# A two-model decoder on one core: order of the weight rounding at its nine boundaries, norm offset, first tile, end and a memory bank

## The reference

```
for l in range(2):
    x = x + 0.5 * rms_norm(swiglu(rms_norm(x)), w)           # ffn1, width 2816
    x = x + rms_norm(parallel_head_groups(rms_norm(x)), w)   # retention + gated DeltaNet ("mix")
    x = x + rms_norm(cross_attention(rms_norm(x), rms_norm(mem)), w)
    x = x + 0.5 * rms_norm(swiglu(rms_norm(x)), w)           # ffn2
h = rmsnorm(x) @ w_in        # second model: Mamba2 branch and dilated attention branch
x = x + (gates0 * y_ssm + gates1 * y_att) @ w_mix_out
x = x + swiglu(rmsnorm(x))
return rmsnorm(x)            # final norm, scaled by norm_final
```

## Time and profile before

| | |
|---|---|
| median of three runs | 1930.05 us |
| the profiled execution's own time | 1928.99 us |
| its span, first to last instruction | 1927.2 us |
| granted TensorE clock, mean | 0.997 of full speed |
| PEld / DVE / ACT / POOL busy | 87% / 37% / 56% / 80% |
| POOL, line 390 (`wlo`) | 1184 instructions, mean 1310 ns, 1501.8 us |
| ACT, line 417, `whi` | 299 instructions, mean 1902 ns |
| the chain that ended last | PE 94%, ACT 3%, DVE 2% of the span |

### The profile page before, as it was taken

One profiled execution on the slowest core, in us unless ns is written; L12 is line 12 of the kernel. 1 busy time (PEld: TensorE's weight loads), 2 busy tenths in 40 slices (PEclk: granted clock), 3 DMA queues, 4 the chain that ended last, 5 costly groups with the idle time before them and its releaser, 6 DMA issues.

```text
span 1927.2 us, 28342 instructions
## 1 busy us (share of the span) xinstructions
PE 1910.8 (99%) x11287; PEld 1683.6 (87%) x11287; DVE 708.3 (37%) x1406; ACT 1087.2 (56%) x1458; POOL 1544.8 (80%) x1227
## 2 busy tenths in 40 slices
PE   9999999999999999999999999999999999999998
PEld 7888899988888888889999888888999998888887
DVE  2221767521211222138574231113676632122112
ACT  6645674456644575456734665446666667545443
POOL 6998786666899799979776759997767787888995
PEclk9999999999999999999999999999999999999999
DMA  8554543143655565555323536555443444545552
GB/s 320 191 193 173 203 148 132 49 179 124 221 195 192 183 228 198 189 183 195 134 88 110 193 113 217 182 192 212 152 158 136 153 154 153 178 177 202 197 187 98
DMA packets 48661, 331.50 MB, mean 172 GB/s; under 512 B 5393, under 2 KB 6289, under 8 KB 10514
## 3 DMA queue, kind: packets, MB, share of 16 engines
q1 hardware_dynamic: 44208, 314.61, 45.1%
q10 hardware_dynamic: 4322, 15.09, 2.2%
HBM read 328.63 MB, written 1.05 MB: 171 GB/s over the span
## 4 chain that ended last, share of the span: by engine, by line
PE 94%; ACT 3%; DVE 2%; ACTq 1%; issue 0%; DVEq 0%; DMA 0%
PE bank L1942 20%; PE bank L1911 16%; PE bank L1912 16%; PE bank L1913 16%; PE bank L1946 10%; ACT arena L417 1%; PE bank L2050 1%; PE bank L2074 1%; PE bank L2386 1%; PE bank L2402 1%; PE bank L2016 1%; PE bank L2052 1%; PE bank L2508 1%; PE bank L2647 1%; PE bank L2487 1%
## 5 line engine op out<-in xcount | busy, mean ns | idle before, releaser
L390 POOL TENSOR_TENSOR wlo<-raw,whi 128x512 fp32r<-128x512 f32 x1184 | 1501.8, 1310 | 332.6 <-ACT whi L417 332.0
L417 ACT ACTIVATE whi<-raw 128x2048 fp32r<-128x2048 f32 (+1 forms) x299 | 568.1, 1902 | 192.0 <-PE bank L1913 156.6
L417 ACT ACTIVATE arena<-bank 128x512 f32<-128x512 f32 (+4 forms) x389 | 210.8, 552 | 439.8 <-PE bank L1946 266.4
L1942 PE MATMUL bank<-uT,whi 128*128 128x512 f32 x1632 | 408.2, 392 | 0.0
L1942 PEld LDWEIGHTS bank<-uT,whi 128*128 128x128 f32 x1632 | 296.3, 189 | 55.0
L1946 PEld LDWEIGHTS bank<-uT,wlo 128*128 128x128 f32 x1632 | 222.6, 190 | 15.9
L1946 PE MATMUL bank<-uT,wlo 128*128 128x256 f32 x1632 | 227.5, 282 | 0.0
L1911 PE MATMUL bank<-uT,whi 128*128 128x256 f32 x768 | 222.6, 290 | 0.3 <-DVE memT L1221 0.3
L1912 PE MATMUL bank<-uT,whi 128*128 128x256 f32 x768 | 217.1, 283 | 0.0
L1913 PE MATMUL bank<-uT,wlo 128*128 128x256 f32 x768 | 217.1, 283 | 0.0
L1911 PE MATMUL bank<-whi,uT 128*128 128x512 f32 (+1 forms) x416 | 160.8, 387 | 0.0
(11 more groups left out here) (315 smaller groups left out, 2698.6 us busy)
## 6 DMA issues: line engine op xcount, KB each, us to landing
raw<-in_w SPq DMA_DIRECT2D x295, 1024.0 KB, 4.8
rows<-in_rows ACTq DMA_DIRECT2D x22, 512.0 KB, 4.9
raw<-in_w SPq DMA_DIRECT2D x4, 512.0 KB, 7.2
arena<-in_mem ACTq DMA_DIRECT2D x2, 1024.0 KB, 9.5
x<-in_x SPq DMA_DIRECT2D x2, 512.0 KB, 5.4
out<-x SPq DMA_DIRECT2D x2, 512.0 KB, 2.7
arena<-in_amask ACTq DMA_DIRECT2D x1, 576.0 KB, 6.1
cst<-in_cst SPq DMA_DIRECT2D x1, 468.0 KB, 10.9
```

The source lines that it names most:

```text
L390: r = pool.tensor_tensor(wlo[n % LAND][:, k], raw[n % LAND][:, k], whi[n % RING][:, k].bitcast(F32), ALU.subtract)
L417: return act.activation(o, i, f, **k)
L1942: pe.matmul(both, w[0][:, c], parts[:, :, k, :], start=start and k == 0, stop=False)
```

## The change

Edit A is in `boundary`: ACT no longer rounds a weight unit between `pre_root(1)` and the rounding of tile 1; it rounds two behind it. Edit B: in `pre_root`, DVE makes mean plus epsilon (`pre_bias`) in place of ACT, and ACT waits for it in front of the root. Edit C: PE gets four more idle products after the first two products of the first tile and two more in the middle of it. Edit D: the last piece of `y_part` goes to bank 4, with a wait for the first `m_ready`, and ACT and DVE take it right behind the other three. Edit E, the end: DVE scales tile 0 in two halves between the adds of tile 1; for tile 1 POOL multiplies one half with the norm weights and ACT scales it, and DVE does the other half, into `ub`; each store starts when both halves of its tile are ready. Edit F: three semaphores of early tables become one (`tables_in`), and `cleared` becomes `pool_side`.

```diff
@@ boundary (ACT) @@
                 pre_root(1)
-                split()
                 u_hi(1)
-                split()
+                split(2)
@@ sum_root (ACT) @@
-                    act.drain()
-                    if h == 0:
+                    d = act.drain()
+                    if h == 0 and done == "rms_pre":
+                        d.then_inc(sems["pre_sum"], 1)
+                    elif h == 0:
                         fn(st[:, c0 + 4 + t:c0 + 5 + t], st[:, c0 + t:c0 + t + 1], AF.Identity, scale=1.0 / n, bias=eps)
+                if done == "rms_pre":
+                    act.wait_ge(sems["norm_dve"], p.count("norm_dve"))
@@ pre_scale (DVE) @@
+            def pre_bias(t):
+                dve.wait_ge(sems["pre_sum"], p.count("pre_sum"))
+                ts(st[:, 52 + t:53 + t], st[:, 48 + t:49 + t], 1.0 / D, EPS, ALU.mult, ALU.add)\
+                    .then_inc(sems["norm_dve"], 1)
             def pre_scale(t, w):
+                pre_bias(t)
@@ first_pair (PE) @@
                     part_phase(wa, 0, a, 0, 0, (0, 1))
+                    idle_products(4)
                     pe.wait_ge(sems["w_hi"], 1)
...
                     lo_phase(wa, a, 0, 0, True)
+                    idle_products(2)
                     pe.wait_ge(sems["u_hi"], p.count("u_hi"))
@@ Mamba part: ACT, DVE, PE @@
-                        hi_parts(mT, (6, 1, 7))
+                        hi_parts(mT, (6, 1, 7, 4))
...
-                    if hp == 2 and g == 2:
-                        hi_parts(mT, (6,), 3)
...
-                        lo_parts(mT, (6, 1, 7))
-                        lo_parts(mT, (6,), 3)
+                        lo_parts(mT, (6, 1, 7, 4))
...
-                    y_part((6,), 3)
+                    pe.wait_ge(sems["m_ready"], p.n["m_ready"] + 1)
+                    y_part((4,), 3)
@@ end: POOL, ACT, DVE @@
+            pool.tensor_tensor(ub[:, 1, 0:512], x[:, 1, 0:512], rows[:, r % 3, 0:512], ALU.mult).then_inc(sems["pool_side"], 1)
...
+            act.wait_ge(sems["pool_side"], DEPTH + 1)
+            act.wait_ge(sems["norm_dve"], p.count("norm_dve"))
+            fn(ub[:, 1, 0:512], ub[:, 1, 0:512], AF.Copy, scale=st[:, 55:56]).then_inc(sems["out_ready"], 1)
...
+            stt(x[:, 0, 0:512], x[:, 0, 0:512], st[:, 54:55], w[:, 0:512], ALU.mult, ALU.mult).then_inc(sems["out_ready"], 1)
+            row_add(1, 0, N_UNITS - 1)
+            stt(x[:, 0, 512:], x[:, 0, 512:], st[:, 54:55], w[:, 512:], ALU.mult, ALU.mult).then_inc(sems["out_ready"], 1)
+            row_add(1, 1, N_UNITS - 1)
+            pre_bias(1)
+            dve.drain()
+            tt(ub[:, 1, 512:], x[:, 1, 512:], w[:, 512:], ALU.mult)
+            dve.wait_ge(sems["rms_pre"], p.count("rms_pre"))
+            dve.reciprocal(st[:, 55:56], st[:, 55:56]).then_inc(sems["norm_dve"], 1)
+            dve.drain()
+            ts(ub[:, 1, 512:], ub[:, 1, 512:], st[:, 55:56], None, ALU.mult).then_inc(sems["out_ready"], 1)
```

More of the change, by code:

```diff
@@ L347, in _ @@
             sp.dma_start(raw[2][:], a["w"][2]).then_inc(sems["raw_landed2"], 16)
-            sp.dma_start(cst[:, P:], a["cst"][:, P:]).then_inc(sems["cst_in"], 16)
-            sp.dma_start(posi, a["pos"].to_broadcast((P, SEQ))).then_inc(sems["pos_in"], 16)
-            sp.dma_start(lvl_f32, a["lvl"]).then_inc(sems["lvl_in"], 16)
+            sp.dma_start(cst[:, P:], a["cst"][:, P:]).then_inc(sems["tables_in"], 16)
+            sp.dma_start(posi, a["pos"].to_broadcast((P, SEQ))).then_inc(sems["tables_in"], 16)
+            sp.dma_start(lvl_f32, a["lvl"]).then_inc(sems["tables_in"], 16)
             for n in range(3, N_UNITS):
@@ L355, in _ @@
                 sp.dma_start(raw[n % LAND][:], a["w"][n]).then_inc(sems[f"raw_landed{n % LAND}"], 16)
-            for t in range(NT):
-                sp.wait_ge(sems["out_ready"], t + 1)
-                sp.dma_start(out[0, t * P:(t + 1) * P, :], x[:, t, :]).then_inc(sems["stored"], 16)
+            sp.wait_ge(sems["out_ready"], 2)
+            sp.dma_start(out[0, 0:P, :], x[:, 0, :]).then_inc(sems["stored"], 16)
+            sp.wait_ge(sems["out_ready"], 4)
+            sp.dma_start(out[0, P:SEQ, :], ub[:, 1, :]).then_inc(sems["stored"], 16)
             sp.wait_ge(sems["stored"], 16 * NT)
@@ L393, in _ @@
                 if n == 8:
-                    pool.wait_ge(sems["cst_in"], 16)
+                    pool.wait_ge(sems["tables_in"], 48)
                     for i, m in enumerate((UI, UI, LI, LI)):
                         pool.tensor_copy(msk4[:, i, :], m)
-                    pool.wait_ge(sems["lvl_in"], 16)
+                    pool.wait_ge(sems["tables_in"], 48)
                     pool.tensor_copy(lvl[:, :], lvl_f32)
@@ L408, in _ @@
                     score_masks()
+            r = N_ROWS - 1
+            pool.wait_ge(sems[f"row_landed{r % 3}"], 16 * (r // 3 + 1))
+            pool.wait_ge(sems["x_part2"], 4 * DEPTH + 2)
+            pool.tensor_tensor(ub[:, 1, 0:512], x[:, 1, 0:512], rows[:, r % 3, 0:512], ALU.mult).then_inc(sems["pool_side"], 1)
         @block.scalar
@@ L1270, in rotary_angles @@
             def rotary_angles():
-                dve.wait_ge(sems["cst_in"], p.count("cst_in", 16))
-                dve.wait_ge(sems["pos_in"], p.count("pos_in", 16))
+                dve.wait_ge(sems["tables_in"], 48)
+                dve.wait_ge(sems["tables_in"], 48)
                 dve.drain()
@@ L1883, in _ @@
             w = use_row()
[L1884 to L1892, removed]
+            row_add(0, 0, N_UNITS - 1)
+            row_add(0, 1, N_UNITS - 1)
+            pre_bias(0)
+            dve.wait_ge(sems["rms_pre"], p.count("rms_pre"))
+            dve.reciprocal(st[:, 54:55], st[:, 54:55])
+            dve.drain()
[6 more added lines that the diff above has]
+            tt(ub[:, 1, 512:], x[:, 1, 512:], w[:, 512:], ALU.mult)
+            dve.wait_ge(sems["rms_pre"], p.count("rms_pre"))
+            dve.reciprocal(st[:, 55:56], st[:, 55:56]).then_inc(sems["norm_dve"], 1)
+            dve.drain()
+            ts(ub[:, 1, 512:], ub[:, 1, 512:], st[:, 55:56], None, ALU.mult).then_inc(sems["out_ready"], 1)
         @block.tensor
@@ L2232, in _ @@
                 if L == 0:
-                    pe.wait_ge(sems["cst_in"], 16)
+                    pe.wait_ge(sems["tables_in"], 48)
                 first_pair((0, 1), ("tok_out", "tok_out"))
```

6 lines of the change are left out of this document (3 added, 3 removed).

## The result

The changed kernel takes 1944.47 us (median; single runs 1940.29 to 1948.15), the kernel before in the same comparison 1929.99. The ratio is 1.0074, 95% interval 1.0062 to 1.0086: slower by 14.5 us where 5.8 were predicted, and outside the range. The four runs were 1940.29, 1941.80, 1947.13 and 1948.15, so the median lies in a gap between two pairs, and no run was near it. The profiled execution took 1941.8, its span is 1940.0.

The account below looks back on a forecast made before the run. PE, 99% busy, was taken as the bound, with POOL next at 80%. +8.1 - 0.8 - 0.8 - 0.8 = +5.7 on the profiled 1928.99 gave 1934.7, or 1935.8 us against the median; range 1931 to 1939.

Parts of the forecast that it names:

- Edit A at mix and cross-attention: Boundaries into mix: PE late on POOL by +2.1 us (first layer) and +2.4 (second); into cross-attention +1.6 each, two times.
- Edit A into feed-forward parts: Into ffn2 twice and from first layer into second: gain and stall cancel, +0.1 us each, 0.3 together.
- Edit A in front of the second model: Boundary before the second model: PE's margins are above 3 us, so the transposes' gain stays, -0.35 us.
- Sum of edit A's late starts: All nine boundaries: +8.1 us net of what PE's transposes gain, bounds 7.0 to 9.2.
- Edits B to E: Transposes' wait: 0.45 us gained once, 0.2 elsewhere, counted within edit A; program start, memory bank and end: -0.8 each.
- the wait that I had named as late next: Row sums' write to bank 4, now waiting for the fourth piece's rest; edit D as a whole put at -0.8 us.
- The third rival, the clock: Clock falls in PE's new waits of about 2 us at four places; one or two falls: 1938.5 to 1942; chance 0.12.
- The step that failed outright: POOL beside DVE's SBUF work at ffn1 to mix: slowed, not fully blocked; a unit takes 6.05 us instead of 5.11.
- Edit F: 0: Early tables' semaphores: the tables land many us before anyone asks, so 0.

Follow-up runs that it names:

- the last two experiments: Changed kernel with the small multiply's operand in PSUM, 1941.84 us; the same plus eight idle products in each of the four long waits, 1940.40 us.
- The last kernel: Changed kernel with the small multiply's operand in PSUM and eight idle PE products in each of the four long waits: 1940.40 us, ratio 1.0051.

## Why the prediction was wrong

The direction and the main place were right; the size was not. Of the 8.7 us between forecast and median, some 2.6 are DVE shut out by POOL, 2.1 late starts priced too low, 1.4 the clock, 1.4 too much gain from B to E, and 1.3 the time at which the clock first rose. By steps:

- **Edit A at mix and cross-attention: right.** Against the kernel without edit A my terms amount to 2.1 + 0.45 and 2.4 + 0.2 for mix (with the gain of edit B, which they had netted) and 1.6 + 0.2 for cross-attention. Measured 2.60, 2.62 and 2.01. POOL started 3.84 behind the transposes, not 3.61, but its first unit at mix was shorter than I took.
- **Edit A into feed-forward parts: mis-sized.** "+0.1 each" plus the lost 0.2 gives 0.3, measured 0.6 to 0.66 each. The 0.23 of POOL's later start is a part of it. The other is a wait that I had passed over: the second unit there (`rows_unit`) also comes late, by 0.28. I had called the third unit the tightest and priced it alone; two margins drawn on by the same delay both have to be worked out.
- **Edit A in front of the second model: the sign was wrong.** "PE's margins are above 3 us there, the gain stays" looked at PE's margins on POOL. PE waited for DVE instead: a small `SCALAR_TENSOR_TENSOR` on SBUF operands took 0.80 to 0.84 us in every profile with edit A at this place and 0.26 to 0.28 without it; POOL now ran beside it, and it ended 0.09 behind POOL's current instruction. +0.56, where my terms come to -0.15.
- **Sum of edit A's late starts**: 10.1 by my terms, 12.2 measured.
- **Edits B to E: too much gain.** I had 2.05 for B, 0.8 each for C, D and E: 4.45. The medians say 3.0. By the starts of the kernel without A and C, the transposes gain 1.5 (0.42 once, about 0.15 at seven others) and D 0.5: the two waits go (-0.84, -0.39), and +0.71 comes back at the row sums, which is the wait that I had named as late next and priced too low. E is -0.73, as forecast. C is 0.6 in the one pair of profiles that shows it, and no time confirms it. A retention wait adds 0.3.
- **The third rival, the clock, came true beside the forecast.** I had given it 0.12 as an alternative; it is an addition. With waits of 1.85 to 2.1 us at four places, the traces hold one fall (changed kernel), two (operand in PSUM), two (edit A alone), one (edit A except in front of the second model) and none where idle products fill them. A wait of 2.09 at 216.12 in the changed kernel was not followed by one, the same wait at 215.89 with the operand in PSUM was. So it is a cost of about 1.5 us a fall that comes in some executions; the 1.4 of the medians rests on five runs each. The Trainium skill (TensorE: Matmul & The Clock Gate, HAM oscillation) was the warning; the price was in the rows, and I kept it out of the sum. The example of the Trainium skill there is a kernel whose clock falls again and again as PE waits; here no more than two of the four waits of an execution were followed by a fall.
- **The step that failed outright** is "full blocking would be far more than the 0.94 us that the rows show, so I go by the rows". The rows were of POOL slowed by DVE, not of DVE shut out by POOL. The Trainium skill (SBUF — State Buffer, its table of terms, shared port pair) has the loser block while the winner holds the ports. The runs show DVE as the loser, blocked not for one POOL instruction but for a whole row of them: 4.9 to 5.0 us at the multiply, 11.7 to 11.8 at the norm product. The sum had nothing for this: 2.6 us in the medians, 5.1 in an execution where the multiply is shut out. And I looked for it only where POOL's work was pushed beside DVE at the boundary, not at what a POOL row shifted against DVE does 10 us further on.
- **Edit F: 0**, nothing in the traces speaks against it.

The sum as measured: -3.0 for B to E, +12.2 for late starts, +1.4 for the clock (the two kernels with the PSUM operand), +2.6 for the multiply (changed kernel less the one with the PSUM operand, 1944.47 - 1941.84; 3.3 by their ratios): 13.2 of 14.5. But 2.6 is a share of the runs and no cost of one execution: the profiled run of the changed kernel, 1941.80, had the multiply at 1.17, and the two runs 5 to 8 us higher fit a multiply that was shut out, though no trace holds them. Also the two lower runs, 1940.29 and 1941.80, lie above the range: the late starts and the clock alone were enough to miss it.

The last 1.3 us are the start of the program. The runs of a kernel fall into two groups about 2 us apart: 1925.89 to 1926.85 and 1928.09 to 1928.29 without edit A (and one run at 1937.17), 1929.1 to 1930.0 and 1931.2 to 1931.8 for the kernel before beside the last two experiments. The profiles show both kinds. In some the granted clock was up for a while from 4.5 to 6.6 us on, before it fell and rose for good; in others it rose first at 13.84 or later. The products that spread the norm weights, without edit A and in the changed kernel:

```profile
5.85 2.03 PE L2253 MATMUL bank<-rows,arena 1*128 1x512 f32 x4
```

```profile
5.85 3.78 PE L2252 MATMUL bank<-rows,arena 1*128 1x512 f32 x4
```

Edit A touches nothing here. Profiles of both kinds exist with edit A; without it the late kind shows in the run times alone. The last kernel's profiled execution is of the late kind (clock up at 14.24) and took 1940.41; less the late group without edit A that is 12.1 to 12.3, the 12.2 of the shifts. So the 1.3 belongs to the mix of executions that a median happened to catch.

Open is why the same multiply is let in after 1.0 us in some runs and after 5 in others: where it was shut out, it was issued 0.12 to 0.14 us after the start of a POOL instruction (the norm product 0.03 and 0.06), where it was let in, 0.15 to 0.30 after, which is too near to be called a reason.

## What to carry to other kernels

When a change delays one engine, price each consumer of the delay and then each engine that will now run beside it for a stretch in which it did not: a margin of PE on POOL says nothing on DVE. A DVE instruction with two SBUF operands, beside an unbroken row of POOL work, is a risk of the whole row's length, be it 32 or 512 columns; for the multiply of 32 columns one operand in PSUM removed it (0.19 us instead of 4.98). A new wait of about 2 us on PE is to be priced with a share of a clock fall behind it, and not as a rival case. Before differences of 1 or 2 us between medians are read, look whether the runs fall into groups, and compare group with group.

## What the runs showed of the hardware

- DVE can be shut out for a whole row of POOL instructions: 4.98 us for 32 columns, 11.79 us for 512 columns across nine instructions of POOL. With an operand in PSUM the multiply of 32 columns took 0.19.
- A drain of POOL behind each of its 1184 subtractions cost the kernel before 65 us (1995.16 against 1929.87), though POOL was only 80% busy.
- Waits of 1.85 to 2.1 us on PE are followed by a stretch at half clock in some cases and not in others that look alike; the fall came with PE already at work again (wait over at 1108.85, clock 0.50 from 1109.52 to 1112.93).
- Where no change of clock is on record yet, the clock column of a window shows full speed; the spacing of the matmuls (0.43 against 0.23 us) is the better witness. So the longer group of runs has the higher mean granted clock on record: without edit A 1.000 in the three of 1928.1 to 1928.3 against 0.998 or 0.999 in the seven of 1925.9 to 1926.9.
